# A second counter behind every row, and a new order for the woven steps, in a layer kernel with gathered experts

## The reference

```
z = rmsnorm(x) @ w_in                       # latent attention and gated linear attention inputs
h = x + concat(rmsnorm(mla(z)), gla(z)) @ w_out
xn = rmsnorm(h)
# peer: 8 heads, each picks 16 of 16384 experts for each token
e    = top 16 of (v1 + v2), of two lists of 16 best keys         # (token, head, 16)
gate = softmax(top scores)
act  = gelu(sum_d xn[t, d] * peer_u[e[t, h, k], d])
h    = h + sum over h, k of gate * act * peer_v[e[t, h, k], :]
y    = h + sigmoid(rmsnorm(h) @ w_ple_gate) * (p @ w_ple_proj)
```

## Time and profile before

| | us |
|---|---|
| three runs | 4484.02, 4472.86, 4484.68 |
| median | 4484.02 |
| the profiled execution, its own time | 4484.02 |
| its span in the trace | 4482.1 |
| TensorE, matmul | 2300.2 busy, 51% |
| VectorE | 3340.5 busy, 75% |
| ScalarE | 469.5 busy, 10% |
| GpSimd | 2183.4 busy, 49% |
| DMA | 1607.69 MB, mean 359 GB/s |

### The profile page before, as it was taken

One profiled execution on the slowest core, in us unless ns is written; L12 is line 12 of the kernel. 1 busy time (PEld: TensorE's weight loads), 2 busy tenths in 40 slices (PEclk: granted clock), 3 DMA queues, 4 the chain that ended last, 5 costly groups with the idle time before them and its releaser, 6 DMA issues.

```text
span 4482.1 us, 23444 instructions
## 1 busy us (share of the span) xinstructions
PE 2300.2 (51%) x8006; PEld 1352.4 (30%) x8006; DVE 3340.5 (75%) x3712; ACT 469.5 (10%) x902; POOL 2183.4 (49%) x1220
## 2 busy tenths in 40 slices
PE   8648994543888754466985239730000470000915
PEld 3326442322456221235773223530000230000401
DVE  0230767889567998986778976689999779987682
ACT  0111102112011000111121200100000100000000
POOL 0000335653331366677676565335566638876360
PEclk9669996556989877666766569875555685555957
DMA  8347899985998999987989899998999999999996
GB/s 297 106 164 257 353 424 357 365 336 227 420 420 341 422 414 420 390 330 320 361 329 406 315 371 399 413 369 336 384 402 366 420 414 422 422 406 421 422 397 212
DMA packets 254477, 1607.69 MB, mean 359 GB/s; under 512 B 28259, under 2 KB 46051, under 8 KB 84310
## 3 DMA queue, kind: packets, MB, share of 16 engines
q0 software_dynamic: 172032, 1244.21, 68.4%
q1 hardware_dynamic: 81014, 352.95, 20.6%
q10 hardware_dynamic: 1312, 9.03, 0.5%
HBM read 1562.98 MB, written 42.56 MB: 358 GB/s over the span
## 4 chain that ended last, share of the span: by engine, by line
PE 34%; DVE 29%; DMA 14%; POOL 13%; issue 6%; ACT 2%; SPq 1%; DVEq 0%; ACTq 0%; POOLq 0%
PE bank L689 20%; POOL ring L2102 11%; DVE ring L1634 10%; DVE total L1659 9%; DMA ring<-in_peer_u,idx_all 5%; PE bank L1014 4%; DMA ring<-in_peer_v,idx_all 2%; POOL front L2084 1%; DMA front<-z_dram 1%; PE bank L897 1%; PE bank L667 1%; DMA front<-in_norm_ple 1%; DVE front L1093 1%; PE bank L800 1%; PE bank L747 1%
## 5 line engine op out<-in xcount | busy, mean ns | idle before, releaser
L2102 POOL DMA_INDIRECT ring<-in_peer_u,idx_all x576 | 1076.5, 1869 | 866.3 <-DVE dots L1634 395.7
L1659 DVE SCALAR_TENSOR_TENSOR total<-ring,gate_all,total 128x2048 f32<-128x2048 f32 x571 | 1342.2, 2351 | 185.1 <-DMA ring<-in_peer_v,idx_all 156.7
L1634 DVE CUSTOM_DVE_ANT_0 ring<-ring,xrow 128x2048 f32<-128x2048 f32 x576 | 1297.7, 2287 | 231.2 <-DMA ring<-in_peer_u,idx_all 227.8
L2102 POOL DMA_INDIRECT ring<-in_peer_v,idx_all x576 | 1006.7, 1748 | 768.7 <-DVE total L1659 326.8
L689 PE MATMUL bank<-front 128*128 128x512 f32 (+3 forms) x2560 | 1108.0, 592 | 81.4 <-ACT front L1764 77.1
L667 PE MATMUL bank<-ident,front 128*128 128x128 f32 (+1 forms) x320 | 68.0, 401 | 1356.2 <-DVE front L1093 1300.2
L689 PEld LDWEIGHTS bank<-front 128*128 128x128 f32 (+1 forms) x2560 | 454.9, 181 | 729.1 <-issue 722.1
L667 PEld LDWEIGHTS bank<-ident,front 128*128 128x128 f32 (+1 forms) x320 | 54.9, 217 | 1372.1 <-DVE front L1093 1297.8
L1014 PE MATMUL bank<-front 128*128 128x128 f32 (+2 forms) x1536 | 258.0, 330 | 21.6 <-DMA front<-in_peer_w_q 17.0
L2062 POOL DMA_DIRECT2D xrow<-xn_dram x6 | 3.6, 594 | 522.4 <-DVEq L1552 522.4
L1014 PEld LDWEIGHTS bank<-front 128*128 128x128 f32 x1536 | 240.0, 192 | 39.5 <-DMA front<-in_peer_w_q 21.7
(11 more groups left out here) (293 smaller groups left out, 2678.3 us busy)
## 6 DMA issues: line engine op xcount, KB each, us to landing
front<-in_w_in SPq DMA_DIRECT2D x96, 980.0 KB
front<-in_w_out SPq DMA_DIRECT2D x48, 1024.0 KB
front<-in_peer_w_q SPq DMA_DIRECT2D x48, 1024.0 KB
front<-in_w_ple_gate SPq DMA_DIRECT2D x48, 1024.0 KB
front<-in_w_uq SPq DMA_DIRECT2D x6, 1536.0 KB, 11.8
ring<-in_peer_u,idx_all POOLq DMA_INDIRECT x576
ring<-in_peer_v,idx_all POOLq DMA_INDIRECT x576
front<-in_x_prompt SPq DMA_DIRECT2D x8, 1024.0 KB, 8.0
```

The lines of the kernel that those rows point to most:

```text
L1634: e.tensor_tensor_reduce(out=ring[:, b, :], in0=ring[:, b, :], in1=xrow[:, t % 2, :], scale=1.0, scalar=0.0, op0=ALU.mult, op1=ALU.add, ac ...
L1659: e.scalar_tensor_tensor(out=total, in0=ring[:, b, :], scalar=c1, in1=total, op0=ALU.mult, op1=ALU.add).then_inc(s("summed"), 1)
L2102: e.indirect_dma_start(out=ring[:, k % RING, :], out_offset=None, in_=a[("peer_u", "peer_v")[side]][0], in_offset=bass.IndirectOffsetOnAxi ...
```

## The change

Two things are changed. First, GpSimd no longer waits for dots_done or summed. After each dot product and after each weighted sum, VectorE waits for that instruction's own semaphore and then raises a new one, buffers_free, with `sem_inc`. It starts at 8 (RING), raised once before the first row, and the gather into slot n waits for n + 1. The wait on summed that stood ahead of each weighted sum now stands behind each one, so three further waits on summed go as well. Second, the three tables have new values, with the same lengths (777, 36 and 16): 658 of 777 values of ROWS_BEFORE differ. Some of them, by what the step does (the row count before which it stands):

The diff, with the tables cut:

```diff
-PAGES_BEFORE = [409, 412, 412, 417, 422, 441, 445, 450, 455, 461, 461, 473, 480, 485, 493, 503]
+PAGES_BEFORE = [380, 381, 384, 392, 396, 403, 406, 419, 430, 432, 437, 445, 446, 457, 463, 469]
...
-    0, 9, 39, 63, 119, 136, 155, 173, 178, 181, 186, 218, 255, 275, 301, 313, 346, 355, 365, 378, 386, 388, 388, 391,
-    391, 391, 404, 406, 406, 406, 406, 406, 406, 407, 456, 470]
+    1, 7, 40, 95, 118, 140, 155, 174, 177, 180, 202, 247, 265, 287, 330, 346, 350, 370, 372, 380, 385, 390, 390, 404,
+    406, 406, 406, 406, 406, 406, 406, 406, 406, 408, 443, 443]
...
@@ -1611,6 +1611,10 @@
                 pass
             for x in first_route(0):
                 pass
+
+
+
+            e.sem_inc(s("buffers_free"), RING)
             weave = woven()
             rows_taken, steps_taken = [0], [0]
 
@@ -1633,6 +1637,8 @@
                     e.wait_ge(s(f"rows_landed{b}"), 16 * (n // RING + 1))
                     e.tensor_tensor_reduce(out=ring[:, b, :], in0=ring[:, b, :], in1=xrow[:, t % 2, :], scale=1.0, scalar=0.0,
                                            op0=ALU.mult, op1=ALU.add, accum_out=dots[:, t % 2, i:i + 1]).then_inc(s("dots_done"), 1)
+                    e.wait_ge(s("dots_done"), u * TOPK + k + 1)
+                    e.sem_inc(s("buffers_free"), 1)
                     row_taken()
 
             def gated(t, lo, hi, n):
@@ -1650,18 +1656,17 @@
                     b, n = k % RING, first_slot(u, 1) + k
                     m = u * TOPK + k
                     c1 = gate_all[:, u * TOPK + k:u * TOPK + k + 1]
-                    if j or k:
-                        e.wait_ge(s("summed"), m)
                     e.wait_ge(s(f"rows_landed{b}"), 16 * (n // RING + 1))
                     if j == 0 and k == 0:
                         e.tensor_scalar(total, ring[:, b, :], c1, None, ALU.mult).then_inc(s("summed"), 1)
                     else:
                         e.scalar_tensor_tensor(out=total, in0=ring[:, b, :], scalar=c1, in1=total,
                                                op0=ALU.mult, op1=ALU.add).then_inc(s("summed"), 1)
+                    e.wait_ge(s("summed"), m + 1)
+                    e.sem_inc(s("buffers_free"), 1)
                     row_taken()
                 if j == PH - 1:
                     xr = xrow[:, t % 2, :]
-                    e.wait_ge(s("summed"), (u + 1) * TOPK)
                     e.wait_ge(s("h_loaded"), 16 * (t + 1))
                     e.tensor_tensor(xr, xr, total, ALU.add).then_inc(s("peer_done"), 1)
 
@@ -1681,7 +1686,6 @@
                 pass
 
             xr = xrow[0:NS, PT % 2, :]
-            e.wait_ge(s("summed"), UNITS * TOPK)
             e.wait_ge(s("h_loaded"), 16 * T)
             link(e.tensor_tensor(xr, xr, total[0:NS], ALU.add))
             e.wait_ge(s("sample_back"), 16)
@@ -2086,19 +2090,12 @@
                                              in_offset=bass.IndirectOffsetOnAxis(ap=page_rows[:, u:u + 1], axis=0))\
                             .then_inc(s(f"pages_landed{u % PAGE_BUFS}"), 16)
 
-            def taken(u, side, k):
-
-                e.wait_ge(s(("dots_done", "summed")[side]), u * TOPK + k + 1)
-
             def gathers(u, side):
 
-                block = GATHERS.index((u, side))
                 for k in range(TOPK):
-                    pages_until(first_slot(u, side) + k)
-                    if k >= RING:
-                        taken(u, side, k - RING)
-                    elif block:
-                        taken(*GATHERS[block - 1], k + TOPK - RING)
+                    n = first_slot(u, side) + k
+                    pages_until(n)
+                    e.wait_ge(s("buffers_free"), n + 1)
                     e.indirect_dma_start(out=ring[:, k % RING, :], out_offset=None, in_=a[("peer_u", "peer_v")[side]][0],
                                          in_offset=bass.IndirectOffsetOnAxis(ap=idx_all[:, u * TOPK + k:u * TOPK + k + 1], axis=0))\
                         .then_inc(s(f"rows_landed{k % RING}"), 16)
```

## The result

The changed kernel takes 4542.01 us (median of 6 runs, 4538.24 to 4550.3) against 4484.35 before (6 runs): ratio 1.0132, 95% interval 1.0113 to 1.015. It is 58 us slower, where 4608 us, 124 slower, were forecast.

What follows compares the result with a forecast made beforehand. VectorE and the DMA engines were both taken as near their end, VectorE alone binding from 3000 to 3501 us. 4484 + 121 (70 + 27 + 24) = 4605, a second way 4616; taken 4608, range 4510 to 4700.

Steps and rivals of the forecast that it cites:

- The price of a row: Behind each row on VectorE: dot products 0.27 us more (2.48), sums 0.13 more (2.50), mean 0.20 us a row.
- VectorE's busy time: Sign to look for: busy time, 3340.5 us before, hardly changes, since the price is idle time between instructions.
- That GpSimd gains and loses nothing: Gather waits on POOL: one per gather before and after, for the same row, so gathers gain no freedom.
- The tail at no cost: The 300 rows from 3501 us on: the price stays under 2.56 us a row, so covered, 0 us.
- the forecast's end of 60: Other end for the 300 rows from 3501 us on: 60 us if they are not covered.
- What lies on the path: Share of 0.20 us a row that is exposed over the run: 70 + 27 + 24 = 121 us, from 70 to 231.
- the half: Rows before 1400 and from 2000 to 3000 us: half of 48 and 53 us counted as paid, 24 and 27.
- The rest of the sum: Rows from 3000 to 3501 us (62 + 115), VectorE 99% busy: 0.20 us each, all of it exposed.
- The second sum: Check from tile 3's routing end on, with the new tables' row counts: 3374 + 1149 + 93 = 4616 us.
- If TensorE's chain keeps that moment: End of tile 3's routing: stays at 3180 us, with 695 rows done by then for 736.
- Rival 1: Only the bare stretches pay, new order saves a little: 4484 + 70 = 4554, down to 4510; chance 0.16.
- Rivals 2, 3 and 4: Every row pays, tail too: 4715 (0.16); price nothing or made good: 4484 to 4495 (0.07); new order removes waits: 4405 (0.09).

Runs made afterwards that it cites:

- own_signal: Kernel before plus a wait and an increment nobody waits for behind all 1152 rows, GpSimd's waits and tables as before: 4538.14 us, ratio 1.0106.
- sync_only: Changed kernel with the three tables of before, so the waits and increments alone: 4541.72 us, ratio 1.0116 against the kernel before.
- from_row_864: Kernel before plus the wait and an increment nobody waits for behind rows 864 to 1151 only: 4491.88 us, ratio 1.0006.
- rows_656_to_863: Kernel before plus the wait and an increment nobody waits for behind rows 656 to 863 only: 4541.52 us, ratio 1.0104.
- order_only: Kernel before with the three new tables, no added waits or increments: 4503.6 us, ratio 1.002.
- tail_four: Kernel before plus a wait and four increments, in place of one, behind rows 864 to 1151: 4542.16 us, ratio 1.0118.
- wait_alone: Kernel before plus a wait without an increment behind the 112 dot products of rows 656 to 863: 4505.88 us, ratio 1.0027.

## Why the prediction was wrong

*The price of a row* was right: 2.48 and 2.50 us from start to start, as forecast, and the rule of the Trainium skill ("VectorE: DVE Perf Modes", section "The DRAIN you can't avoid") that a semaphore after each instruction costs nothing was rightly set aside for the waits: with the wait alone it is 2.33 for 2.21. A semaphore that the instruction itself raises is another matter: every dot product of the kernel before raises dots_done, and they follow each other in 2.21. The mean of 0.20 is 0.22 where every row pays. VectorE's busy time, forecast to hardly change, rose by 46 us.

*That GpSimd gains and loses nothing* was right (own_signal against sync_only).

*The tail at no cost* was right: 3 us for 288 rows, and the forecast's end of 60 for it is what a row 0.2 us too slow would cost.

*What lies on the path* is the step that failed, in the term of rows before tile 3's first routing. In this, with the old tables that the sum was made for, the forecast took "172 rows from 1400 to 2000" as hardly covered since VectorE was 92% busy, 34 us, and half of the price of 505 rows in the two stretches around it, 51 us: 85 in all. Rows 0 to 655 cost 8. With the new tables the traces put 22 there, still a quarter of it. The reason given for the half, that idle time on TensorE and ScalarE is paid once more, was wrong as well: the delay at row 323 was 28 us and at row 669 it was 9. A stretch without idle time is a bound only if what it delays is not waiting for something else later. The rest of the sum, 177 rows from 3000 to 3501 at 0.20 = 35 us, was too small, 47 were measured for rows 656 to 863. 8 + 47 + 3 = 58 is the sum of the three parts; all rows together gave 48 (own_signal) and 52 (sync_only), which the intervals allow.

*The second sum*, which seemed to confirm the first, had an error of its own: "If TensorE's chain keeps that moment". That moment was the end of the whole routing, 3180 us, and the chain does not keep it. What precedes it, from tile 3's first routing on, is VectorE's own work, 67 rows and the steps between, 195 us in the kernel before; with 38 rows it takes 139, by the forecast's own prices 195 - 29 x 2.30 + 38 x 0.20 = 136. So it ended at 3125, not at 3180 nor at 3156 to 3225. Nor is the 2985 of both kernels shown to be a moment that the chain keeps: with the new tables alone it is 2964. From 3125 the sum was right: 196 us to tile 4's routing (194 forecast) and 1144 from there to the last sum's start at 4465 (1149 forecast). It missed the profiled execution's 4558 by 58 us, of which 55 are this moment. So the agreement of two sums at 4605 and 4616 was luck, two different errors of nearly one size.

*The rivals.* Rival 1, that only the bare stretches pay, is what happened, with one bare stretch and not two, and no help from the order (its 4554, down to 4510, holds the 4542). Its 70 us for 349 rows come near in part by luck: 172 of these rows pay almost nothing with the old tables, and the other stretch pays more than its 35. Rivals 2, 3 and 4 are out by from_row_864, by rows_656_to_863 and by order_only. That the new tables by themselves give nothing is shown; their 9 us of loss is small beside the spread, if clear of it. The kernel order_only starts its last part 21 us earlier (first routing at 2963.55) with 12 rows less, ends tile 4's routing 222 us earlier with 101 rows less, and then has 402 rows for 301 at the pace of the transfers.

## What to carry to other kernels

Before a price per instruction is multiplied by a count, find the last moment at which the engine still waits for someone else: what lies ahead of it can be nearly free (8 us for 656 rows here with the old tables), and what lies behind it up to the next full resource is paid in full. The first half holds for one order of the work and has to be looked at again for another: with the new tables the traces show some 22 us ahead of that moment. A high busy share doesn't show this; the same two moments of the chain in two traces do. And two ways to the same number confirm it only if they don't share the view of what sets the pace.

## What was not expected of the hardware

An increment of a semaphore, recorded at 0.02 us, holds VectorE's queue for 0.09 us when it follows another one (tail_four), and for 0.15 behind a wait (wait_alone against the changed kernel). GpSimd's issue of a gather grew: in the kernel before its mean was 1.87 us for peer_u and 1.75 for peer_v, in the changed one 1.93 and 1.92 by the same groups of the page:

```profile
L2099 POOL DMA_INDIRECT ring<-in_peer_u,idx_all x576 | 1111.9, 1930 | 833.6 <-DVEq L1641 418.3
...
L2099 POOL DMA_INDIRECT ring<-in_peer_v,idx_all x576 | 1107.8, 1923 | 742.7 <-DVEq L1666 314.3
```

That the slower row is the cause is not shown: the means are 1.83 and 1.86 with the new tables alone (order_only), and 1.84 and 1.86 with the waits alone (sync_only).
